# The mixers' layer norm: where the squares lie, who adds them, and how many chunks TensorE sums

## The reference, cut to what matters

```
y = concat([y_a, y_b, y_c, y_d]) * silu(g_lat)
x_new = layer_norm(alpha * x + gate[:, None] * (y @ w_out), ln_g, ln_b)

def layer_norm(x, g, b):
    mu = mean(x)                     # over the 1024 features
    var = mean((x - mu) ** 2)
    return (x - mu) * rsqrt(var + 1e-5) * g + b
```

## Time and profile before

| | |
|---|---|
| median of three runs | 3222.96 us |
| the profiled execution, its own time | 3227.86 us |
| its span | 3226.1 us |
| PE busy | 3092.9 us (96%) |
| PEld (weight loads) busy | 2363.3 us (73%) |
| DVE (VectorE) busy | 1436.1 us (45%) |
| POOL (GpSimd) busy | 1443.8 us (45%) |
| ACT (ScalarE) busy | 1152.7 us (36%) |
| mean granted TensorE clock | 0.985 |

### The profile page before, as it was taken

The page is one execution under the profiler, slowest core; times in us unless marked ns, Lnnn a source line. Parts: engine busy times, 40 slices in busy tenths (PEclk is TensorE's granted clock), DMA queues, the critical chain, the costliest instruction groups (busy, mean ns, idle before and its releaser), DMA issues.

```text
span 3226.1 us, 55094 instructions
## 1 busy us (share of the span) xinstructions
PE 3092.9 (96%) x20586; PEld 2363.3 (73%) x20586; DVE 1436.1 (45%) x2950; ACT 1152.7 (36%) x1975; POOL 1443.8 (45%) x2267
## 2 busy tenths in 40 slices
PE   8999989999999999999999999998999998989998
PEld 6888767888778886777768877766666676657665
DVE  3232464222542225444452223666466435665754
ACT  3222433222332224111242223555445435555554
POOL 4555665555655556333255545343144122342423
PEclk9999999999999999999999999999999998999999
DMA  4222423222342224111142243200010211111111
GB/s 151 98 98 97 136 93 131 95 97 98 112 155 97 94 96 144 59 59 59 47 143 94 96 143 103 81 28 28 27 35 28 73 53 66 41 34 40 34 61 59
DMA packets 74359, 264.76 MB, mean 82 GB/s; under 512 B 7856, under 2 KB 9136, under 8 KB 73904
## 3 DMA queue, kind: packets, MB, share of 16 engines
q1 hardware_dynamic: 69584, 246.02, 22.8%
q10 hardware_dynamic: 4576, 15.98, 1.4%
HBM read 252.53 MB, written 7.34 MB: 81 GB/s over the span
## 4 chain that ended last, share of the span: by engine, by line
PE 86%; DVE 7%; ACT 3%; issue 2%; POOL 1%; DMA 0%; DVEq 0%; SPq 0%; ACTq 0%; POOLq 0%
PE ps L1764 29%; PE ps L1793 19%; PE ps L1769 14%; PE ps L2379 3%; PE ps L2352 2%; PE ps L2402 2%; PE ps L1983 1%; PE ps L2246 1%; PE ps L1757 1%; PE ps L2185 1%; PE ps L2432 1%; PE ps L2266 1%; DVE tb L3093 1%; PE ps L2469 1%; PE ps L2108 1%
## 5 line engine op out<-in xcount | busy, mean ns | idle before, releaser
L1227 POOL TENSOR_TENSOR wl<-raw,wh 128x256 fp32r<-128x256 f32 x1604 | 1176.3, 766 | 1463.4 <-ACT wh L1349 838.5
L1377 ACT ACTIVATE wh<-raw 128x1024 fp32r<-128x1024 f32 x224 | 237.8, 1062 | 945.3 <-PE ps L1769 862.8
L1764 PE MATMUL ps<-xh,wh 128*128 128x512 f32 x1344 | 523.0, 389 | 2.0 <-ACT pr L1455 2.0
L1764 PE MATMUL ps<-xl,wh 128*128 128x512 f32 x1344 | 522.8, 389 | 0.0
L1349 ACT ACTIVATE wh<-raw 128x1024 fp32r<-128x1024 f32 x177 | 187.4, 1059 | 430.4 <-PE ps L1793 279.8
L1769 PE MATMUL ps<-xh,wl 128*128 128x512 f32 x1344 | 331.9, 389 | 0.0
L1764 PEld LDWEIGHTS ps<-xh,wh 128*128 128x128 f32 x1344 | 252.3, 188 | 55.1 <-issue 2.8
L1764 PEld LDWEIGHTS ps<-xl,wh 128*128 128x128 f32 x1344 | 252.3, 188 | 52.4
L1769 PEld LDWEIGHTS ps<-xh,wl 128*128 128x128 f32 x1344 | 252.3, 188 | 52.3
L1764 PE MATMUL ps<-ah,wh 128*128 128x512 f32 x732 | 287.6, 393 | 0.8 <-DVE al L2701 0.8
L1764 PE MATMUL ps<-al,wh 128*128 128x512 f32 x732 | 286.3, 391 | 0.0
(11 more groups left out here) (415 smaller groups left out, 4962.7 us busy)
## 6 DMA issues: line engine op xcount, KB each, us to landing
raw<-wts_dram SPq DMA_DIRECT2D x458, 512.0 KB, 3.5
spilled_dram<-hc ACTq DMA_DIRECT2D x1, 3072.0 KB, 10.7
hc<-spilled_dram ACTq DMA_DIRECT2D x1, 3072.0 KB, 9.9
tb<-tab_dram ACTq DMA_DIRECT2D x5, 512.0 KB, 3.7
spilled_dram<-hc ACTq DMA_DIRECT2D x1, 2048.0 KB, 7.2
hc<-spilled_dram ACTq DMA_DIRECT2D x1, 2048.0 KB, 9.7
out_dram<-hc SPq DMA_DIRECT2D x8, 256.0 KB, 2.1
hc<-x_dram SPq DMA_DIRECT2D x7, 256.0 KB, 6.7
```

What stands on the lines that cost most here:

```text
L1227: ins = pool.tensor_tensor(lo, src, hi.bitcast(F32), ALU.subtract)
L1377: act.activation(wh[:, slot_of(n + 2), :], raw[:, at % RAW, :], ACT.Copy).then_inc(hi_done, 1)
L1764: pe.matmul(out_, weight(wh, s, k), x_(k, at), start=first, stop=False)
```

## The change

`lnsq` gets eight places instead of two, so ScalarE writes all eight squares without waiting for TensorE. GpSimd adds squares 1, 2 and 3 onto square 0. VectorE adds square 7 onto square 6. TensorE multiplies four chunks instead of eight, in the order 4, 5, 0 (the sum of four), 6 (the sum of two), and signals ScalarE once, at the end. Three semaphores are new.

```diff
+LN_ADDED = 4
         def lnsq(k):
-            return area(k % 2 * TOK, TOK)
+            return area(k * TOK, TOK)
# GpSimd
+            def add_ln_squares(layer):
+                n = out_tiles(layer) * P
+                for k in range(1, LN_ADDED):
+                    pool.wait_ge(lnsq_ready, layer * KC + k + 1)
+                    if k > 1:
+                        pool.wait_ge(ln_added, layer * (LN_ADDED - 1) + k - 1)
+                    pool.tensor_tensor(lnsq(0)[:, 0:n], lnsq(0)[:, 0:n], lnsq(k)[:, 0:n], ALU.add).then_inc(ln_added, 1)
...
                 if name == "mixers":
                     mixers(*rest)
+                if name == "mix":
+                    add_ln_squares(*rest)
# ScalarE
                 for k in range(KC):
                     get(d2a, "d2a")
-                    if k >= 2:
-                        get(p2a, "p2a")
                     n_tok = out_tiles(layer) * P
-                    give(act.activation(lnsq(k)[:, 0:n_tok], hc[:, k, 0:n_tok], ACT.Square), a2p, "a2p")
-                get(p2a, "p2a", 2)
+                    act.activation(lnsq(k)[:, 0:n_tok], hc[:, k, 0:n_tok], ACT.Square).then_inc(lnsq_ready, 1)
+                get(p2a, "p2a")
# TensorE
-                for k in range(KC):
-                    get(a2p, "a2p")
+                for k in [*range(LN_ADDED, KC - 2), 0, KC - 2]:
+                    if k == 0:
+                        pe.wait_ge(ln_added, (layer + 1) * (LN_ADDED - 1))
+                    elif k == KC - 2:
+                        pe.wait_ge(ln_paired, layer + 1)
+                    else:
+                        pe.wait_ge(lnsq_ready, layer * KC + k + 1)
                     for b, (at, w) in enumerate(runs(n_tok)):
-                        ins = pe.matmul(ps[:, 6 + b, 0:w], ones, lnsq(k)[:, at:at + w], start=k == 0, stop=k == KC - 1)
-                    give(ins, p2a, "p2a")
+                        ins = pe.matmul(ps[:, 6 + b, 0:w], ones, lnsq(k)[:, at:at + w], start=k == LN_ADDED, stop=k == KC - 2)
+                give(ins, p2a, "p2a")
# VectorE
                 dve.wait_ge(d2a, c.at("d2a"))
+                dve.wait_ge(lnsq_ready, (layer + 1) * KC)
+                dve.tensor_tensor(lnsq(KC - 2)[:, 0:n], lnsq(KC - 2)[:, 0:n], lnsq(KC - 1)[:, 0:n], ALU.add).then_inc(ln_paired, 1)
                 get(a2d, "a2d")
```

More of the change, by code:

```diff
@@ L961, in build @@
         osq_ready, orms_full, orms_ready, orms_used = sem("osq_ready"), sem("orms_full"), sem("orms_ready"), sem("orms_used")
+        lnsq_ready, ln_added, ln_paired = sem("lnsq_ready"), sem("ln_added"), sem("ln_paired")
         late_full, late_taken = sem("late_full"), sem("late_taken")
```

## The result

The changed kernel takes 3231.8 us (median of 18 runs, 3224.3 to 3237.5), the kernel before 3224.8 us beside it (18 runs, 3219.5 to 3233.5). The ratio is 1.0016 (95% interval 1.0008 to 1.0023): about 5 us slower, small and real (the two medians lie 7.0 us apart, the two means 5.4).

What follows compares the result with a forecast made beforehand. TensorE was taken to bound the kernel, holding 86% of the chain. Layer 0's -1.4 us, layer 1's +1.6 us and 0 behind the stage made +0.2 us on the median of 3222.96, so 3223.2 us, range 3217.4 to 3228.9.

Steps and rivals of the forecast that it cites:

- What bounds the kernel: Whole kernel: TensorE holds 86% of the chain; the change works on only 20.0 us, in both layers' products with squares.
- the chunk's price: TensorE's products in both stages: 1.29 us a chunk in layer 0, 0.86 in layer 1 at 2.4 GHz, twice at 1.2.
- the first squares: ScalarE's squares, paced by VectorE 0.86 and 0.60 us apart; TensorE starts on number 4 at 2679.3 and 3210.6.
- GpSimd's adds: GpSimd's three adds of squares in each layer: 2.10 us each in layer 0, 1.40 us in layer 1.
- The collision: VectorE's pair add falls on GpSimd's third add in both layers, costing GpSimd's sum 0.77 us, bounds 0 and 0.96.
- The clock: After both new idle times, 5.4 and 3.9 us, TensorE starts at 1.2 GHz; rise expected 4.1 us after the start.
- The sum of the stages: Products with squares in both layers: -1.4 us in layer 0, +1.6 us in layer 1, together +0.2 us.
- Behind the stage ... nothing is late: Phase after layer 0's stage: weight tiles split later and loads some 20 us later cost 0 us, kept between -2 and +2.4.
- Rival 4: Late-split tiles starve the next phase, or time moves somewhere these stages don't show: over 10 us; chance 0.05.
- Rivals 1 to 3: Clock does not matter, 3221.4 us, 0.15; low clock lasts longer, 3228.5 us, 0.15; adds slow beside VectorE, 3227.1 us, 0.10.
- The base: Whole kernel before the change: median 3222.96 us, to which +0.2 us was added; its runs already reached 3228.8 us.

Runs made afterwards that it cites:

- e5: The changed kernel run again without edits; ratio 1.0019 to the kernel before.
- e3: The kernel before with 64 tiny fp32 products (256 TensorE instructions) added at the end of layer 0's mix; ratio 1.0034 to the kernel before.
- e6: The change in layer 1's mix alone, layer 0 as in the kernel before; ratio 1.0001 to the kernel before.
- e1: The changed kernel with 8 tiny fp32 products (32 TensorE instructions) added at the end of layer 0's mix; ratio 0.9991 to the kernel before.
- e2: The kernel before with 56 tiny fp32 products (224 TensorE instructions) added at the end of layer 0's mix; ratio 1.0026 to the kernel before.
- e7: The change in layer 0's mix alone, layer 1 as in the kernel before; ratio 1.0011 to the kernel before.
- e10: The changed kernel with 8 tiny fp32 products added in layer 1's mix, ahead of the products with squares; ratio 1.0009 to the kernel before.
- e13: The kernel before with 56 quick small products (224 instructions) in idle time behind layer 0's mix; ratio 1.0013 to the kernel before.
- e9: The changed kernel with TensorE summing six chunks, first square first, plus four tiny products in layer 0's mix; ratio 0.9992 to the kernel before.
- e14: The kernel before with 64 quick small products (256 instructions) in idle time behind layer 0's mix; ratio 1.0000 to the kernel before.
- e8: The changed kernel with eight fp32 products of a constant on TensorE between mean and first square, both layers; ratio 0.9991 to the kernel before.

## Why the prediction was wrong

*What bounds the kernel, the chunk's price, the first squares:* right. TensorE started 5.38 and 3.83 us after the mean (5.4 and 3.9 forecast), squares came 0.86 us apart, and chunks cost 1.29 us at 2.4 GHz.

*GpSimd's adds:* 1.82 and 1.27 us, where 2.10 and 1.40 were taken. *The collision* was put on the wrong instruction: some 0.36 us more for VectorE's add, 0.72 us for the piece that GpSimd starts next, nothing on GpSimd's sum, and the sum wasn't the last wait in the trace after, since TensorE at 1.2 GHz still had chunk 5 to do.

*The clock:* right in layer 0, half wrong in layer 1, where TensorE began at 2.4 GHz and the low clock lasted 3.4 us, not to the end. That makes +0.1 us instead of +1.6. In other executions of the same code there was no fall at all (e5: PEclk 1.00 throughout, 8.2 us). e3 shows the same for layer 0 of the old code (12.5 us instead of 14.2).

*The sum of the stages* was +0.2 us; the trace says -1.5. Layer 0's part agrees within 0.2 us, but with some luck: not GpSimd's sum set its end, as forecast, but TensorE's own pace.

*"Behind the stage ... nothing is late"* is the step that failed. I followed GpSimd, the loads and VectorE past the stage, but not TensorE's own code: removing products was counted as time saved and not as code that moves. The long stop stands in all three profiles of the changed kernel, at the same product, and in none of the other 17. With a low clock beside it the stretch is 4.5 to 5.3 us longer. The low clock isn't all the stop's doing: it came after it in two of the profiles, but in e5 it began at 2806.98, 2.5 us ahead of the stop. The term for what lies behind the stage was 0, with bounds of -2 and +2.4. Measured are 4.5 us in the stretch and 0.9 us ahead of it (104.6 us from the first activation of 1/sigma to the stretch, 103.7 before), with -1.5 in the stages and -0.3 in the rest 3.6 us from the mean of layer 0 on. The measured loss averages 1.0013 over the three comparisons, some 4 us. Rival 4 was the right one, "the time moves somewhere that these stages don't show", but it had 0.05, a price of over 10 us and no mechanism, so the range, drawn from the other three, was too narrow. Rivals 1 to 3 all put the time in the stages, and the loss wasn't there.

*The base:* the three runs of before had a median 1.8 us under that of the 18 beside the changed kernel. Runs of one kernel scatter over 14 us; the range took the three runs' spread for all of it.

What is shown: the loss comes with layer 0's part (e5 against e6), not from the stages; the stop stands at a place of the code that moves with it, 16 records for 32 instructions, and where it is long a load of code began 2 us late. What is supported, not shown: that this stop is the measured loss. For it are e1, the times by placement, and the longer stretch. What stays open: why that load is late in the changed kernel, and why e2, e7, e10 and e13, whose TensorE code lies the same at that product, stopped for 0.2 to 0.53 us only, while e7, e10 and e13 measured 1.0009 to 1.0013. It may be long in some executions only. Code that all 20 share does so: a burst in layer 0's mixers (at 2136 us in the kernel before, where it is 0.76 us) stops for 0.43 to 0.99 us in 14 profiles and not in six. Or the place of the whole program matters too. Two more profiles with a stretch of 40 us and no long stop there (e9, e14) show that a fall of the clock alone costs 2.6 to 3 us in it. And one profile is a weak judge: the untouched code from the stretch to layer 1's mean took 371.6 to 378.3 us in the 20.

## What to carry to other kernels

Where a kernel is a long unrolled program and a burst of tiny products runs at some 70 records in a microsecond, deleting instructions upstream can change the burst: compare the same instruction's time in both traces all the way to the end, not only the stage that was edited, and try a few pads before judging an edit worth 1 or 2 us. Here, work taken off TensorE in a stage that waits for others came back in part as a lower clock (in layer 0, 3.6 us of TensorE's 7.2 at 1.2 GHz, before 3.4 of 12.3); starting it with the first input (e9), or keeping it busy while it waits (e8), made the stages shorter than halving its work did. When a pad is meant to be free, price it from a row of the same shape first.

## What was not expected of the hardware

- Three profiles of one program stop for 1.74 to 2.29 us at the same product, with no wait that the profile shows, and a 16 KB load of code that began 2 us late. The kernel before has 0.19 us 16 records earlier, in its one profile.
- An fp32 product of 4 columns with a full 128x128 stationary operand costs as much as 0.33 us in a row of 56 (18.64 us, at a mean granted clock of 0.65), and 77 of the records of 64x32 products take 1.05 us together.
- Of two colliding adds, the one that started later paid: VectorE's grew by 0.35 to 0.37 us, GpSimd's by nothing. GpSimd's next piece, started beside VectorE's add, took twice its 0.72 us, as two pieces of the tile at the earlier trace rows had (1.46 and 1.52 us).
- Up to layer 0's `mix` all 20 profiles run the same code, and they reach it up to 3.9 us earlier and 8.4 us later than the kernel before: a span read from one profile can't judge 5 us.
